# Token mixers of a hybrid decoder: outputs normalised straight out of PSUM, states scaled ahead by ScalarE, and a new order of steps

## The reference

```python
def layer(x, ...):                       # dims: D_MODEL 1024, CHUNK 128
    x = x + mixing(rmsnorm(x), ...)[0]
    x = x + cross_attn(rmsnorm(x), mem_k, mem_v, w_xq, w_xo)
    return x + swiglu(rmsnorm(x), w_gate, w_up, w_down)

# retention, one chunk (gla: decay by channel and token, in the exponent)
s = einsum('bhid,bhjd->bhij', qc, kc) * decay        # gamma**(i-j), causal
o = einsum('bhij,bhjv->bhiv', s, vc) + einsum('bhid,bhdv->bhiv', qc, S) * q_decay
S = S * chunk_decay + einsum('bhjd,bhjv->bhdv', kc * k_decay, vc)
# mlstm, one chunk
s = einsum('bhid,bhjd->bhij', qc, kc) * exp(D - m_tok[..., None])
h = num / maximum(abs(den), exp(-m_tok))[..., None]
C = C * scale[..., None, None] + einsum('bhjd,bhjv->bhdv', kc * wk, vc)
# each mixer's output
o = head_rmsnorm(o, g) * silu(gate)      # o * rsqrt(mean(o*o) + EPS), per head
out = concat([o_r, o_g, o_m]) @ w_out
```

## Time and profile before

| | |
|---|---|
| time, median of 3 runs | 2277.98 us (2274.43 to 2282.07) |
| time of the profiled execution | 2289.77 us |
| its span | 2287.8 us |
| PE busy | 2037.1 us (89%) |
| DVE busy | 938.2 us (41%) |
| POOL busy | 726.6 us (32%) |
| ACT busy | 626.3 us (27%) |
| bytes moved by DMA | 219.81 MB |

### The profile page before, as it was taken

The page is one execution under the profiler, slowest core; times in us unless marked ns, Lnnn a source line. Parts: engine busy times, 40 slices in busy tenths (PEclk is TensorE's granted clock), DMA queues, the critical chain, the costliest instruction groups (busy, mean ns, idle before and its releaser), DMA issues. The chain is left out here.

```text
span 2287.8 us, 35847 instructions
## 1 busy us (share of the span) xinstructions
PE 2037.1 (89%) x14140; PEld 1908.2 (83%) x14140; DVE 938.2 (41%) x1301; ACT 626.3 (27%) x840; POOL 726.6 (32%) x356
## 2 busy tenths in 40 slices
PE   5999858689889999999799996786998999999995
PEld 5899647489679999999779984674994999999994
DVE  4543676624314330332173366774343243203313
ACT  4311542023323221222251126210323232212221
POOL 3333311323123334333343332122330233333331
PEclk9999967889999999999899997767999999999997
DMA  5432101225432222222343320013236122222221
GB/s 213 148 114 84 57 0 51 83 79 188 168 121 75 87 83 89 84 84 83 113 147 128 102 74 33 1 51 119 103 139 240 65 75 84 84 93 83 83 86 51
DMA packets 61270, 219.81 MB, mean 96 GB/s; under 512 B 10612, under 2 KB 11288, under 8 KB 58792
## 3 DMA queue, kind: packets, MB, share of 16 engines
q1 hardware_dynamic: 60216, 214.32, 26.1%
q10 hardware_dynamic: 880, 3.11, 0.4%
HBM read 202.47 MB, written 11.40 MB: 93 GB/s over the span
## 5 line engine op out<-in xcount | busy, mean ns | idle before, releaser
L954 POOL TENSOR_TENSOR WL<-RAW,WH 128x1024 fp32r<-128x1024 f32 (+1 forms) x276 | 645.1, 2337 | 1221.2 <-ACT WH L995 1221.2
L571 PE MATMUL PS<-XH,WH 128*128 128x288 f32 x2880 | 622.4, 298 | 18.4 <-DVE XL L1292 10.1
L571 PE MATMUL PS<-XH,WL 128*128 128x288 f32 x2880 | 618.9, 297 | 0.0
L571 PE MATMUL PS<-XL,WH 128*128 128x288 f32 x2880 | 618.9, 297 | 0.0
L995 ACT ACTIVATE WH<-RAW 128x1024 fp32r<-128x1024 f32 x276 | 292.3, 1059 | 1093.0 <-PE PS L571 1065.3
L571 PEld LDWEIGHTS PS<-XH,WH 128*128 128x128 f32 x2880 | 466.8, 190 | 24.1 <-issue 21.1
L571 PEld LDWEIGHTS PS<-XL,WH 128*128 128x128 f32 x2880 | 466.8, 190 | 0.0
L571 PEld LDWEIGHTS PS<-XH,WL 128*128 128x128 f32 x2880 | 466.8, 190 | 0.0
L571 PE MATMUL PS<-HH,WH 128*128 128x288 f32 x704 | 151.2, 296 | 4.1 <-DVE FT L1919 4.1
L571 PE MATMUL PS<-HH,WL 128*128 128x288 f32 x704 | 150.8, 296 | 0.0
L571 PE MATMUL PS<-HL,WH 128*128 128x288 f32 x704 | 150.7, 296 | 0.0
(11 more groups left out here) (259 smaller groups left out, 2474.7 us busy)
## 6 DMA issues: line engine op xcount, KB each, us to landing
RAW<-in_w_gu SPq DMA_DIRECT2D x88, 512.0 KB, 3.4
RAW<-in_w_dn SPq DMA_DIRECT2D x48, 512.0 KB, 3.4
RAW<-in_w_in SPq DMA_DIRECT2D x44, 512.0 KB, 3.5
KV<-in_cache_k SPq DMA_DIRECT2D x32, 512.0 KB, 7.1
KV<-in_cache_v SPq DMA_DIRECT2D x32, 512.0 KB, 7.3
RAW<-in_w_xk SPq DMA_DIRECT2D x16, 512.0 KB, 4.6
RAW<-in_w_xv SPq DMA_DIRECT2D x16, 512.0 KB, 3.4
RAW<-in_w_v SPq DMA_DIRECT2D x16, 512.0 KB, 3.4
```

Source lines behind the costliest of these rows:

```text
L571: return nc.tensor.matmul(out, lhsT=lhsT, rhs=rhs, start=start, stop=stop)
L954: nc.gpsimd.tensor_tensor(WL[:, s, w], RAW[:, r, w], WH[:, s, w].bitcast(f32), ALU.subtract).then_inc(split_done.sem, 1)
```

## The change

- **Order of steps.** Retention and gla of the four prompt chunks first, then the mLSTM steps mixed with the sample steps. AT gives the place of a step.
- **PE.** `scores` and `keys` run one step ahead. The product that adds to the state is a function of its own, `new_state`, ahead of `outputs`; `outputs` of chunk 0 leaves out the (empty) state. Retention's scores use the two heads' rows of KT and QT directly, so only gla and mLSTM of the prompt (APART) need QE.
- **Outputs.** ACT squares the outputs in PSUM; DVE reduces and makes mean plus EPS; POOL does only the power; DVE scales PSUM into OC. mLSTM's denominator enters as EPS times its square, retention's query decay and half of its key decay enter as row factors: the decay matrix RD becomes the causal mask times a factor per key, built by ACT once per layer, EPSR is EPS times the factor's square, and QD and the scaled queries QI of retention are gone.
- **States.** Two copies, ST[0] and ST[1], used in turn: ACT writes the scaled state of the next chunk (`scale_state`), and DVE adds the two diagonal halves of the new term.
- **gla keys.** The exponent is taken by ACT in 12 operations on 128 elements straight from GB, with the reference point as bias.
- **Samples.** ACT spreads the sample values into KT's or QT's prompt part (`spread_values`, 8 operations a group); QB has two buffers, zeroed by POOL ahead of time; SBD and SC are asked for earlier.
- **Norms.** In `next_norm` behind "out" and "xo", the last block is left out of the first loop; `features(..., frees=True)` tells ACT through x_free, block by block, that XH and XL may be overwritten while the last output block runs.

```diff
-STEPS = [(c, g) for c in range(NC + 1) for g in range(3)]
+STEPS = [(0, 0), (0, 1), (1, 0), (1, 1), (2, 0), (2, 1), (3, 0), (3, 1),
+         (0, 2), (NC, 0), (1, 2), (NC, 1), (2, 2), (3, 2), (NC, 2)]
+AT = {step: n for n, step in enumerate(STEPS)}
+APART = [n for n, (c, g) in enumerate(STEPS) if c < NC and g > 0]
+SCALED = [n for n, (c, g) in enumerate(STEPS) if 0 < c < NC]
...
-                sp.wait_ge(mb_done.sem, mb_done.at(l, 9))
+                sp.dma_start(SC[:, :, :, :], t["sc"][l, :, 0:3]).then_inc(sc_loaded.sem, 16)
+                sp.wait_ge(ma_done.sem, ma_done.at(l, AT[NC - 1, 1] + 1))
                 stand_alone(sp)
-                sp.dma_start(SC[:, :, :, :], t["sc"][l, :, 0:3]).then_inc(sc_loaded.sem, 16)
                 sp.dma_start(SBD[:, :, :, :], t["sbd"][l, :, 0:3]).then_inc(sbd_loaded.sem, 16)
-                sp.wait_ge(pre_sub.sem, pre_sub.at(l, 4))
...
+                stand_alone(sp)
+                sp.dma_start(SBD[:, :, :, :], t["sbd"][l, :, 3:6]).then_inc(sbd_loaded.sem, 16)
+                sp.wait_ge(st_done.sem, st_done.at(l, AT[NC, 0] + 1))
+                stand_alone(sp)
+                sp.dma_start(o["s_st"][l, :, 0:3], SC[:, :, :, :]).then_inc(sc_stored.sem, 16)
+                sp.wait_ge(sc_stored.sem, sc_stored.at(l, 16))
...
                             last = three(outs, wh, wl, hi, lo, k == 0, k == KB - 1)
+                            if frees and b == stop - 1 and k < KB - 1:
+                                last.then_inc(x_free.sem, 1)
...
                             for i in range(4):
                                 w = slice(32 * i, 32 * i + 32)
-                                mm(both[:, :, w], KG[:, p, i, :], QE[:, s % 2, p, :, w], True, True)
...
+                        for e in range(2):
+                            r = slice(64 * e, 64 * e + 64)
+                            k = KGS[r, p, :] if grp == 1 else KT[r, p0 + p, t0:t0 + L]
+                            mm(bank(q + e, CH * p, L)[0:L], k, QT[r, p0 + p, t0:t0 + L], True, True)
...
+                        if c < NC:
+                            last = mm(bank(q + 2, 2 * W * p, 2 * W), KTT[:, par, 128 * p:128 * p + 128],
+                                      V[:, c, value_at(grp, p, 0, W):value_at(grp, p, 0, W) + 2 * W], True, True)
...
+                            last = mm(bank(q + p)[64 * e:64 * e + 64], k, own_values(grp)[:, 2 * p + e, :], True, True)
...
+                    last.then_inc(u_done.sem, 1)
...
+                        if 0 < c < NC:
+                            queries = (QT if grp == 0 else QI)[:, p0 + p, t0:t0 + L]
...
-                            last = mm(bank(q + 2, 2 * W * p, 2 * W), KTT[:, par, 128 * p:128 * p + 128],
...
-                for i in range(len(STEPS) + 3):
+                scores(0)
+                keys(0)
+                for i in range(len(STEPS) + 2):
+                    if i + 1 < len(STEPS):
+                        scores(i + 1)
+                        keys(i + 1)
+                    if i >= 2:
+                        back(i - 2)
                     if i < len(STEPS):
-                        scores(i)
-                    if 3 <= i:
-                        back(i - 3, i)
-                    if i < len(STEPS):
-                        keys(i)
-                    if 1 <= i <= len(STEPS):
-                        outputs(i - 1)
+                        new_state(i)
+                        outputs(i)
 
...
                 stand_alone(pool)
-                nc.gpsimd.tensor_tensor(KDG[:, :, :], KDG[:, :, :], KT[:, 3:6, :], ALU.mult).then_inc(kdg_ready.sem, 1)
+                nc.gpsimd.tensor_tensor(KDG[:, :, 0:SEQ], KDG[:, :, 0:SEQ], KT[:, 3:6, 0:SEQ], ALU.mult).then_inc(kdg_ready.sem, 1)
...
-                        own_values(nc.gpsimd, group, 0).then_inc(pool_step.sem, pool_step.tick())
-                        own_values(nc.gpsimd, group, 1).then_inc(vb_ready.sem, 1)
...
-                    nc.gpsimd.tensor_scalar(small("ms", n, par)[0:L], small("ss", n, par)[0:L],
-                                                          1.0 / 64, EPS, ALU.mult, ALU.add).then_inc(pool_step.sem, pool_step.tick())
-                    pool.wait_ge(pool_step.sem, pool_step.at(l))
                     stand_alone(pool)
                     nc.gpsimd.tensor_tensor(small("pw", n, par)[0:L], small("ms", n, par)[0:L],
...
                     for k in range(KB - 1):
+                        act.wait_ge(x_free.sem, x_free.at(l, (KB - 1) * (n - 1) + k + 1))
                         x_upper(name, k)
-                        if k == 2:
-                            upper(stage, 7 + SPLIT_SLOTS)
...
+                for h in range(6):
+                    do(RD[:, h, :], CMASK[:, :], ACT.Copy, scale=KDI[:, h:h + 1])
+                    last = do(RDS[:, h, :], CMASKS[:, :], ACT.Copy, scale=KDI[0:64, 6 + h:7 + h])
+                last.then_inc(rd_ready.sem, 1)
...
+                    for p in range(3):
+                        for i in range(4):
+                            last = do(KG[:, p, i, :], GB[:, p, CH * c:CH * c + CH], ACT.Exp, scale=-1.0 / 16,
+                                      bias=small("gref", 1, 16 * p + 4 * c + i))
...
+                        for p in range(n):
+                            decay = (COLS[:, COL["cd"] + p:COL["cd"] + p + 1], small("gcd", 1, 12 * p + c),
+                                     small("mscale", 1, 12 * p + c))[grp]
+                            last = do(state((c + 1) % 2, p0 + p, 1)[:, 0, :], state(c % 2, p0 + p, 1)[:, 0, :], ACT.Copy, scale=decay)
+                        last.then_inc(st_scaled.sem, 1)
...
+                    for b in range(4 * half, 4 * half + 4):
+                        last = do(own_values(grp)[:, :, 64 * b:64 * b + 64], v, ACT.Copy,
+                                  scale=COLS[0:64, COL["batch"] + b:COL["batch"] + b + 1])
...
+                queries_apart(1)
+                for i in range(len(STEPS)):
+                    c, grp = STEPS[i]
...
+                    queries_apart(i + 2)
...
-                    decay_keys(i + 3)
+                    if grp == 1 and c + 1 < NC:
+                        decay_keys(c + 1)
+                    scale_state(i)
+                    act.wait_ge(mb_done.sem, mb_done.at(l, i + 1))
+                    w = 65 if grp == 2 else 64
+                    do(KTT[0:L, i % 2, 0:128 * n].rearrange("p (h v) -> p h v", h=2 * n),
+                       bank(4 * (i % 2) + 3, 0, 2 * n * w)[0:L].rearrange("p (h v) -> p h v", h=2 * n)[:, :, 0:64],
+                       ACT.Square).then_inc(sqo_ready.sem, 1)
+                    for g, before in ((0, AT[NC - 1, 1]), (1, AT[NC, 0]), (2, AT[2, 2])):
+                        if before <= i < before + 2:
+                            spread_values(g, i - before)
...
                         add_to_x(stage, b)
                         if b >= 1:
                             add_square(l, sq_ready, sq_used, n, b - 1)
                     for k in range(KB - 1):
                         x_rest(n, name, k)
+                    add_to_x(stage, KB - 1)
                     x_rest(n, name, KB - 1)
+                    add_square(l, sq_ready, sq_used, n, KB - 2)
                     add_square(l, sq_ready, sq_used, n, KB - 1)
...
+                    dve.wait_ge(kg_exp.sem, kg_exp.at(l, c + 1))
+                    for p in range(3):
+                        last = stt(KG[:, p, :, :], KG[:, p, :, :], CAP,
...
+                    V_.tensor_reduce(ss, KTT[0:L, par, 0:64 * n].rearrange("p (h v) -> p h v", h=n),
+                                     AX.X, ALU.add).then_inc(dve_step.sem, dve_step.tick())
...
+                        stt(den, den, EPS, den, ALU.mult, ALU.mult).then_inc(dve_step.sem, dve_step.tick())
+                        dve.wait_ge(dve_step.sem, dve_step.at(l))
+                        last = stt(ms, ss, 1.0 / 64, den, ALU.mult, ALU.add)
...
+                            last = stt(ms, ss, 1.0 / 64, EPSR[0:L, at:at + 6], ALU.mult, ALU.add)
...
-                    last.then_inc(sm_ready.sem, 1)
...
+                    dve.wait_ge(pw_ready.sem, pw_ready.at(l, s + 1))
...
-                    if grp < 2:
-                        V_.tensor_copy(OC[0:L, par, 0:384], bank(q + 3, 0, 384)[0:L]).then_inc(oc_ready.sem, 1)
...
-                        tt(small("den", 4, 2)[0:L], od[:, :, 64], small("den", 4, 2)[0:L], ALU.max).then_inc(dve_step.sem, dve_step.tick())
...
-                        dve.wait_ge(dve_step.sem, dve_step.at(l))
-                        tt(OC[0:L, par, 0:256].rearrange("p (h v) -> p h v", h=4), od[:, :, 0:64],
-                                              spread(small("den", 4, 2)[0:L], [L, 4, 64], 2), ALU.mult).then_inc(oc_ready.sem, 1)
+                    tt(OC[0:L, par, 0:64 * n].rearrange("p (h v) -> p h v", h=n),
+                       bank(4 * par + 3, 0, w * n)[0:L].rearrange("p (h v) -> p h v", h=n)[:, :, 0:64],
```

(48 more changed lines are left out.)

509 lines of the change are left out of this document (238 added, 271 removed).

## The result

The changed kernel takes 2250.99 us (median of 4 runs, 2246.2 to 2252.14) against 2276.2 for the kernel before: ratio 0.9885, 95% interval 0.9855 to 0.9916. Six more runs in a later group gave 2243.12 (0.9856, 0.9829 to 0.9884; the kernel before took 2276.51 there). So it is faster by 25 to 33 us, where the forecast said 72 (2206, range 2174 to 2236). The sign was right and the size less than half.

The account below looks back on a forecast made before the run. It took the token-mixer loops to be bound by a relay of PE and DVE, with the clock as penalty. Terms 27 + 23 + 5.8 - 0.8 + 16 + 1 gave 72 us saved, a median of 2206, range 2174 to 2236.

Parts of the forecast that it names:

- the term of the clock: Loop over the steps: 10 us added per layer for half-clock stretches in the mixed steps and for extra handovers.
- a relay of 127: Loop over the steps, per layer: PE and DVE handing work to each other at full clock, ideally 127 us.
- if the clock stays near 0.75: Loop over the steps: a stated sign of being wrong; the forecast expected a granted clock above 0.85.
- the stretch ahead of the loop: Before the first scores: no KG subtraction and no wait for a QE, 2.9 us saved a layer.
- the building of RD: Ahead of the loop: 12 small ACT operations delay ACT's evacuation of v, costing 0.4 us a layer.
- the wait of 7.4 us ahead of the third sample step: In the loop: PE's 7.4 us standing goes, as own values no longer stand behind DVE and POOL.
- DVE's work in a prompt chunk: In the loop: DVE's busy time per prompt chunk falls from 18.8 to about 14 us.
- The pairs: Prompt steps of the loop: one retention and one gla step together take 14.5 us, PE working 12 of them.
- Rival 2: Loop: clock low for about a third (150 us), or exponents at or above their upper bound; 2232 us, chance 0.2.
- The norms: Behind out and xo: 4 us saved at each of four, 16 in all, of 5.5 lost at each.
- The start-up: Start of the kernel: loads of RD and QD vanish ahead of the first ACT operation, 1.1 us saved once.
- The base: Whole kernel: profiled execution of 2289.8 us less 72 gives 2218, scaled by 0.5% to a median of 2206.

Follow-up runs that it names:

- the fillers: Changed kernel plus products of no use in PE's waits for gla keys (chunks 1 to 3) and transposed keys of three mLSTM steps: 2217.42 us, 0.9726 of the kernel before.
- the old order: Changed kernel with steps again by chunk, sample steps last, everything else of the change kept: 2220.71 us, 0.9763 of the kernel before.
- their own run: Kernel before with only the two norms behind out and xo made block by block: 2267.49 us, 0.9970 of the kernel before.

## Why the prediction was wrong

The step that failed is the term of the clock: "I add 10 us: the mixed steps hold stretches of 3 us with PE idle, so some of them will be met at the half clock", which made a loop of 137 out of a relay of 127. The loops took 148.5, so the term was 21 and not 10, twice: 23 us of the 32 by which the traces fell short. The forecast kept the clock's cost to the mixed steps, "once or twice". The trace of layer 1 shows a granted clock of 0.75 in the prompt steps and 0.73 in the mixed ones, and a time 9.4 and 12.6 us over the relay. That this is the clock, and not the handovers counted in the same term, the fillers show for 11 to 15 of the 21 us: they leave every chain of the other engines as it was. How the rest divides stays open. The forecast had named the sign of it: wrong "if the clock stays near 0.75".

- *The relay itself* held. The exponents took 3.61, the multiplication 1.89, the stretch ahead of the loop gained 2.9 as forecast (the 0.4 for the building of RD does not show), the wait of 7.4 us ahead of the third sample step went, and no load or store of the samples shows among PE's waits. (DVE's work in a prompt chunk was added up wrongly, 18.8 - 8.1 + 2.3 is 13.0 and not "about 14", but the sum of the time does not use it.) With the waits filled and the clock at 0.87 to 0.88 the loops were 133.6, and 129.8 in one case.
- *The pairs* were forecast 14.5 apart and were 16.6 to 17.6 (ends of retention's outputs at 1428.6, 1446.2, 1462.8 and 1479.5), by the half clock between, as the windows above show. "PE's own work in a pair is 12 us of 14.5, so the thin stretches are no longer than 1.5 us" was wrong twice. The pair's idle time is not spread; it stands in one piece ahead of the gla scores. And the clock fell after stretches whose only long idle piece was 1.65 us.
- *Rival 2* (low clock, the loop at 150) was what happened to the loops, with a chance of 0.2; its length was right, its "about a third" at the low clock was half. It gave 2232 and not 2251, since it kept the norms at 16 and the base as it was.
- *The norms* were mis-sized, 16 for 6.3 by the traces and 7 (2 to 11) by their own run: the loss of 5.5 held the statistics' matmul, and two waits of 1.25 and 0.47 were left.
- *The start-up*, 1.1 for 0.2: the two loads went, but ACT's first DMA issue began at 11.03 us in place of 9.80. Why it did is open.
- *The base.* The profiled execution of before (2289.8, clock 0.933) was near the slowest of all its executions; they went from 2262.6 at 0.947 to 2291.7 at 0.933, while the profiled one of the changed kernel was near its median. The forecast scaled all by 0.5%. If those 12 us lay in stretches at the half clock, and the change rebuilds those, they were in the saving that it counted. That is argued, not shown; the medians differ by 25 to 33 where the traces differ by 40.
- *What the forecast did not ask* was what each part is worth beside the others. It priced the wait for the keys inside the new order, and 2.8 us of sample values ahead of an exponent, and added them up without setting the same relay in the old order beside it. That comparison would have shown both chains mostly covered there.

What stays open: why fillers give nothing in the kernel before, and how much of the gain of each of the other parts (outputs from PSUM, scaled states) is whose; they were not run alone. All of them together in the old order are worth 56 us.

## What to carry to other kernels

When a change reorders steps, follow for each operand the chain of small operations on the engines that are "mostly idle": how many steps lie between the one that frees it and the one that needs it. A two-thirds idle engine was the cause of both waits here, by what stood ahead of one exponent and by a signal given after twelve operations where four would do. And where the clock follows PE's load, price a wait by more than its length: here 6 us of waits a layer were worth 15 on average. An average of busy time over a stretch does not tell whether its idle time is in one piece.

## What the runs showed of the hardware

- Filling PE's waits of 1.7 to 3.6 us with about a hundred useless instructions a layer made the kernel 26 to 30 us faster (granted clock 0.74 to 0.87 in the loop). In the kernel before, about fifty of them in waits of 1.0 to 1.4 us gave nothing (ratio 1.0011).
- The clock fell to the half behind a stretch of 10.2 us in which PE was busy for 7.8 and its longest idle piece was 1.65 us; at the half clock PE was busy without a gap.
- An ACT operation on 128 elements shows 388 ns by itself, but twelve in a row, each of which begins before the one ahead has ended, took 3.61 us, 0.30 each.
- The same code took 145.0 and 148.7 us in the two loops of one execution (granted clock 0.77 and 0.74), and one execution of the kernel before differs from another by up to 29 us, with the granted clock of the whole span (0.947 and 0.933).
